# Pre-norm factors applied to the products instead of the operands, post-norm factors made on columns, in a two-layer transformer block kernel

## The chip, the cores and the metric

One core of one Trainium2 chip runs the whole program once. The metric is the device time in microseconds (us). Lower is better. A profiled execution gives the rows quoted here; its span is the time from its first to its last recorded instruction.

## The reference, cut to what matters

The program computes a first block (two layers, 512 tokens, model width 1024) and a second block, of which only its opening, which follows the first, matters here. With `rms_norm(x, g) = x * rsqrt(mean(x*x) + eps) * g` over the 1024 features of a token, the first block is:

```python
for l in range(2):
    g = norm_gains[l]
    if l == 0:
        mix = dilated_mixer(rms_norm(h, g[0]), w_qkv_a[l], w_o_a[l], cos, sin)
    else:
        kvf = rms_norm(h, kv_norm) @ w_kvf          # keys, values, forget gates
        mix = fox_mixer(rms_norm(h, g[0]), w_q_b[0], w_o_b[0], k, v, cumsum(log_sigmoid(f + b_f)))
    h = h + rms_norm(mix, g[1])
    f = conv_ffn(rms_norm(h, g[2]), w_up[l], conv_w[l], conv_b[l], w_down[l])
    h = h + rms_norm(f, g[3])
```

So there are norms ahead of a projection (pre-norms) and norms of a mixer's or a feed-forward's output (post-norms). `conv_ffn` projects to 5632 channels, applies a causal convolution of width 3 along tokens, then gelu(gate) times value, and projects back.

## The kernel before, in words

**Layout.** The residual `h` and every operand of a projection lie feature-major: eight tiles k = 0..7 of 128 features by 512 tokens. A product of fp32 numbers is made of three fp32r matmuls (`hi_lo_product`): operand and weight are each split into a rounded part (hi) and a rest (lo), and hi*hi, hi*lo and lo*hi are summed in PSUM. A matmul of 128x128 weights with 512 columns is the unit of TensorE's work; one output chunk of a projection from 1024 features takes 24 of them.

**Weights.** SyncE loads units of 128x1024 weights into a ring of four; GpSimd (`split_units`, L476 to L484) splits each unit into hi (L482) and lo (L484), in three slots. It may refill a slot once the last product that reads it is done (`product_done`). TensorE takes each unit with a wait on `part_ready`.

**Products.** `fm_linear` gives feature-major chunks in banks f % 4. Where its operand is still being made, it takes the first three chunks together, k by k, as their operand tiles become ready (the lead), and so holds all three weight slots to the lead's end. `tm_linear` gives token-major blocks (values of the attention), unit by unit, two k to a unit, four token blocks in banks 0 to 3.

**Norms.** In a pre-norm ScalarE squares each `h[k]` (`squares`, L580), TensorE sums them over the features with a matmul by ones into bank 7 (`sum_squares`, L610), ScalarE takes the square root (L614), VectorE the reciprocal on 128x512 (L619). Then `norm_dve` makes h * g * rstd (L626), ScalarE rounds it to hi (`split_act`, L499) and VectorE subtracts to lo (`split_dve`, L504). Products start after that. In a post-norm (`out_dve`, `out_act`, `out_pe`) the squares of the mixer's output `mix` are added on VectorE (L598), summed by one matmul (L603), then root and reciprocal as above, and VectorE updates h tile by tile (L674, L678). The matmuls by ones, and the small ones of one column (L1204), are plain fp32.

**Stages.** Attention a (start: `mixa_*`): rotated queries and keys (twelve chunks, each with a rotation matmul L945 of the copy `nb[0:2]` in bank 4 or 5), values, attention, output projection; feed-forward 0; attention b (`mixb_*`): values in two halves b_v0 and b_v1, forget gates b_f, then keys and queries b_kq pair by pair, which also fill gaps of the attention; output projection; feed-forward 1; second block. Each feed-forward has two halves: 22 chunks up (ScalarE tap L719, VectorE taps L740 and L743, gelu, product L749, splits) and eight chunks down over eleven k (`down`, 33 matmuls each), beside which VectorE works at the second block's modulation vectors (L1196, summed by L1204).

**Order.** Every engine's order is written out by hand in these functions; an engine works in that order, and waits on semaphores stand ahead of single instructions. Nothing is scheduled by a planner.

## Time and profile before

| | us |
|---|---|
| median of 3 runs | 2685.9 |
| lowest, highest | 2664.63, 2690.1 |
| time of the profiled execution | 2680.04 |
| its span | 2678.3 |
| TensorE busy in the span | 2370.1 |
| VectorE, ScalarE, GpSimd busy | 1396.6, 591.2, 1105.2 |

The busy times say how full an engine is, not which wait ends last. That is read stage by stage, from the chain of waits and from the order of instructions in time. Granted clock is given as a share of 2.4 GHz. Where a line number is named without more, it is that of the kernel before.

### The profile page before, as it was taken

What the parts mean: (1) busy time and instruction counts of PE and PEld (TensorE: products, weight loads), DVE (VectorE), ACT (ScalarE), POOL (GpSimd) and SP (SyncE); (2) the same over time, 40 slices, a digit from 0 to 9 for tenths busy, and PEclk for the clock granted to TensorE, in tenths of its full rate; (3) what the DMA queues carried; (4) which work ended last, traced back from release to release, by engine and by line L of the source; (5) the groups of instructions that cost most, each with busy time, mean ns of one, the idle gap of its engine ahead of it and who ended that gap; (6) DMA issues with size and microseconds to landing.
All of it is one profiled execution on the core that took longest, in us unless ns stands there. A gap on an engine that the chain in (4) does not pass through costs nothing.

```text
span 2678.3 us, 34115 instructions
## 1 busy us (share of the span) xinstructions
PE 2370.1 (88%) x14068; PEld 1899.8 (71%) x14068; DVE 1396.6 (52%) x2005; ACT 591.2 (22%) x1159; POOL 1105.2 (41%) x632
## 2 busy tenths in 40 slices
PE   7998799999699996999996989658688796899998
PEld 5866588887477774888883567547488785688886
DVE  5455557446733346465566531677945464550431
ACT  2052220121232322210211300302533321210110
POOL 4613367666342222667662103503210024456663
PEclk9999899999799998999997999868888877999999
DMA  4201134335121111334345001102110001222321
GB/s 154 95 24 48 45 97 173 103 110 184 49 71 40 46 34 39 104 133 149 95 163 203 24 16 49 63 1 77 34 49 3 2 1 55 65 93 95 105 93 63
DMA packets 54058, 204.12 MB, mean 76 GB/s; under 512 B 6000, under 2 KB 6128, under 8 KB 52880
## 3 DMA queue, kind: packets, MB, share of 16 engines
q1 hardware_dynamic: 52560, 188.34, 21.5%
q0 software_dynamic: 1344, 13.60, 1.3%
q8 instruction: 112, 1.84, 0.3%
q14 instruction: 42, 0.34, 0.0%
HBM read 197.72 MB, written 4.19 MB: 75 GB/s over the span
## 4 chain that ended last, share of the span: by engine, by line
PE 81%; DVE 14%; ACT 3%; issue 1%; POOL 1%; DMA 0%; DVEq 0%; SPq 0%; POOLq 0%; ACTq 0%
PE bank L493 59%; PE bank L781 3%; PE bank L809 2%; PE bank L610 1%; DVE nb L619 1%; PE bank L1339 1%; PE bank L1359 1%; PE bank L796 1%; PE bank L2020 1%; PE bank L1367 1%; PE bank L2005 1%; DVE nb L1911 1%; PE bank L2262 1%; PE bank L2016 1%; PE bank L785 1%
## 5 line engine op out<-in xcount | busy, mean ns | idle before, releaser
L493 PE MATMUL bank<-xn_r,parts_r 128*128 128x512 f32 (+1 forms) x3104 | 979.5, 394 | 48.5 <-DVE big_r L504 13.2
L493 PE MATMUL bank<-big_r,parts_r 128*128 128x512 f32 x3112 | 900.5, 393 | 1.0 <-POOL parts_r L484 1.0
L482 POOL TENSOR_SCALAR parts_r<-ring 128x1024 fp32r<-128x1024 f32 x297 | 337.4, 1136 | 1193.8 <-PE bank L493 1169.3
L484 POOL TENSOR_TENSOR parts_r<-ring,parts_r 128x1024 fp32r<-128x1024 f32 x297 | 743.2, 2503 | 24.7
L493 PEld LDWEIGHTS bank<-xn_r,parts_r 128*128 128x128 f32 x3104 | 591.9, 193 | 176.4 <-issue 41.6
L493 PEld LDWEIGHTS bank<-big_r,parts_r 128*128 128x128 f32 x3112 | 584.7, 189 | 123.7 <-DVE big_r L504 2.7
L740 DVE SCALAR_TENSOR_TENSOR big<-bank,small,big 128x511 f32<-128x511 f32 x88 | 65.9, 749 | 277.1 <-ACT big L719 277.1
L719 ACT ACTIVATE big<-bank,small 128x512 f32<-128x512 f32 x88 | 68.3, 781 | 497.1 <-PE bank L493 497.1
L2403 DVE TENSOR_TENSOR big<-big 128x512 f32<-128x512 f32 x32 | 82.3, 2573 | 69.9 <-ACT big_r L2384 69.9
L2357 DVE SCALAR_TENSOR_TENSOR h<-bank,vecs,h 128x512 f32<-128x512 f32 x24 | 17.8, 750 | 193.3 <-PE bank L493 193.3
L493 PE MATMUL bank<-parts_r,xn_r 128*128 128x384 f32 x352 | 95.3, 353 | 15.5 <-DVE big L1902 9.6
L2295 POOL TENSOR_TENSOR big<-big 64x384 f32<-64x384 f32 x12 | 9.9, 822 | 216.9 <-PE bank L2047 164.7
L868 DVE CUSTOM_DVE_ANT_0 big<-bank,cst 128x128 f32<-128x128 f32 (+3 forms) x112 | 54.4, 491 | 85.0 <-PE bank L785 48.8
L610 PE MATMUL bank<-nb,base 128*128 128x512 f32 x112 | 64.9, 728 | 35.5 <-ACT nb L580 35.5
L1196 DVE SCALAR_TENSOR_TENSOR big<-cst,vecs,big 128x1024 f32<-128x1024 f32 x42 | 93.7, 2257 | 2.0 <-DMA cst<-mod_w 1.0
L493 PE MATMUL bank<-mix_r,parts_r 128*128 128x512 f32 x224 | 89.0, 398 | 0.0
L781 PE MATMUL bank<-big 64*128 64x128 f32 (+3 forms) x224 | 81.0, 466 | 0.6 <-issue 0.6
L493 PEld LDWEIGHTS bank<-parts_r,xn_r 128*128 128x128 f32 x352 | 67.8, 201 | 17.8 <-DVE big L1902 10.2
L749 DVE TENSOR_TENSOR big<-big 128x512 f32<-128x512 f32 x44 | 79.5, 1806 | 0.8 <-ACT big L726 0.8
L1902 DVE SCALAR_TENSOR_TENSOR big<-bank,small,big 128x488 f32<-128x488 f32 (+5 forms) x108 | 68.3, 636 | 20.5 <-ACT big L1857 17.3
L610 PEld LDWEIGHTS bank<-nb,base 128*128 128x128 f32 x112 | 22.3, 224 | 78.1 <-issue 38.7
L809 PEld LDWEIGHTS bank<-big 128*128 128x128 f32 x560 | 72.6, 191 | 5.1 <-issue 0.4
(349 smaller groups left out, 2985.4 us busy)
## 6 DMA issues: line engine op xcount, KB each, us to landing
ring<-weights SPq DMA_DIRECT2D x297, 512.0 KB, 3.5
...
```

What stands on the lines that cost most here:

```text
L482: pool.tensor_scalar(rounded(w_hi[:, slot]), w, 1.0, 0.0, ALU.mult, ALU.add).then_inc(sem("hi_ready"), 1)
L484: pool.tensor_tensor(rounded(w_lo[:, slot]), w, value(w_hi[:, slot]), ALU.subtract).then_inc(part_ready, 1)
L493: mm = pe.matmul(ps, rounded(w[a]), rounded(x[b]), start=(start and n == 0), stop=(stop and n == 2))
L610: pe.matmul(bank[7][:, :], ones, sq[:, k % 2], start=(k == 0), stop=(k == KD - 1)).then_inc(summed, 1)
L719: act.activation(cv[:, i % 4], bank[i % 4][:, :], ACT.Identity, bias=gain(f"cb{l}", 2 * KH * s + i), scale=gain(f"cw{l}2", 2 * KH * s + i))\
L740: link(dve, dve.scalar_tensor_tensor(out=c[:, 1:T], in0=ps[:, 0:T - 1], scalar=gain(f"cw{l}1", w), in1=c[:, 1:T], op0=ALU.mult, op1=ALU.add))
L749: dve.tensor_tensor(ff_lo[:, j - 1], ge[:, (j - 1) % 2], cv[:, (2 * j - 1) % 4], ALU.mult)\
L781: mm = pe.matmul(ps[:, 0:w], qT[r:r + HD, hd // 2 % ring, tb * P:(tb + 1) * P], kT[r:r + HD, hd // 2 % ring, 0:w], start=True, stop=(sel i ...
L809: mm = pe.matmul(ps[:, g * HD:(g + 1) * HD], PT[:, t % 2, g, kb * P:(kb + 1) * P], vT[:, kb, hd * HD:(hd + 1) * HD], start=(kb == 0), stop ...
L1196: ins = dve.scalar_tensor_tensor(out=acc, in0=w, scalar=c, in1=acc, op0=ALU.mult, op1=ALU.add)
L1902: ins = dve.scalar_tensor_tensor(out=u[:, :, o0:o1], in0=ps[:, :, o0 + s:o1 + s], scalar=gd_tap(kind, f, j), in1=u[:, :, o0:o1], op0=ALU.m ...
L2403: dve.tensor_tensor(ff2_lo[:, f], ff2_lo[:, f], ff2_lo[:, f], ALU.mult).then_inc(sem("mlp_sq"), 1)
```

## The change

- **Pre-norms of the first block.** The operand of a projection is now h * g, without the factor rstd of each token: ScalarE makes hi from h and the gain (`feed_act`), VectorE makes lo = h * g - hi in one instruction (`feed_dve`), for each tile as soon as it is there. The matmuls that sum squares stand between the products (argument `each`): after the three products of each k of a lead, or after each unit of b_v0. The factor is multiplied in behind the product: into the rotation tables of queries and keys of a, into the copies of the values by ScalarE (`token_rs`, one factor per token, made by four small matmuls and a copy), by an instruction of VectorE in place in PSUM for each of the 88 up chunks (`scale`), and for keys, queries and gates of b by VectorE where ScalarE copied before.
- **Post-norms.** The sums of squares are made on columns: four token blocks of one column each, two small matmuls for each; root and reciprocal work on 128x4; four matmuls of a broadcast column by the identity spread it to 128x512 in bank 5, from where VectorE reads it.
- **Order.** In `out_dve` each h[k] is followed by the lo part of tile k - 1. In the up halves VectorE's taps of a chunk follow the scaling of the next. The gates b_f come ahead of b_v1. b_x's hi and lo follow behind the second reciprocal. The first two copies of keys and queries come behind the cumulated gates.

```diff
     out += ffn(0)
     key_query = np.stack([fm_units(wf[:, :D]), fm_units(i["w_q_b"][0])], axis=1).reshape(-1, P, UNIT)
-    out += [("b_v0", tm_units(wf[:, D:D + 512])), ("b_v1", tm_units(wf[:, D + 512:2 * D])),
-            ("b_f", fm_units(pad_cols(wf[:, 2 * D:], [P], B_HEADS))), ("b_kq", key_query),
+    out += [("b_v0", tm_units(wf[:, D:D + 512])), ("b_f", fm_units(pad_cols(wf[:, 2 * D:], [P], B_HEADS))),
+            ("b_v1", tm_units(wf[:, D + 512:2 * D])), ("b_kq", key_query),
             ("b_o", fm_units(i["w_o_b"][0]))]
     out += ffn(1)
...
+        def token_rstd_pe(pe, norm, n):
+
+            pe.wait_ge(rstd_ready, NORMS.index(norm) + 1)
+            grab(pe, 6, sem("token_rs"), n + 1)
+            for tb in range(TB):
+                mm = pe.matmul(bank[6][:, tb:tb + 1], rstd[:, tb * P:(tb + 1) * P], ident[:, 0:1], start=True, stop=True)
+            mm.then_inc(sem("token_rs_ps"), 1)
+
+        def token_rstd_dve(dve, n):
+            dve.wait_ge(sem("token_rs_ps"), n + 1)
+            dve.tensor_copy(token_rs, bank[6][:, 0:TB]).then_inc(sem("token_rs"), 1)
...
+        def post_rstd_pe(pe, st):
+
+            n = POSTS.index(st)
+            ps = grab(pe, 5, *after(st + "_tmp", KD))
+            pe.wait_ge(post_squared, (n + 1) * KD)
+            for tb in range(TB):
+                pe.matmul(ps[:, tb:tb + 1], sq[:, 1, tb * P:(tb + 1) * P], ones[:, 0:1], start=True, stop=False)
+                if tb == 0:
+                    pe.wait_ge(post_added, ADDS * (n + 1))
+                mm = pe.matmul(ps[:, tb:tb + 1], var[:, tb * P:(tb + 1) * P], ones[:, 0:1], start=False, stop=True)
+            mm.then_inc(sem("post_sum"), 1)
+            pe.wait_ge(sem("post_col_rs"), n + 1)
+            for tb in range(TB):
+                mm = pe.matmul(ps[:, tb * P:(tb + 1) * P], col_rs[:, tb:tb + 1].broadcast_to((P, P)), ident, start=True, stop=True)
+            mm.then_inc(sem("post_rs"), 1)
+
+        def post_rstd_act(act, st):
+            act.wait_ge(sem("post_sum"), POSTS.index(st) + 1)
+            act.activation(col_sd, bank[5][:, 0:TB], ACT.Sqrt, bias=gain("eps"), scale=1.0 / D).then_inc(sem("post_sd"), 1)
+
+        def post_rstd_dve(dve, st):
+            n = POSTS.index(st)
+            dve.wait_ge(sem("post_sd"), n + 1)
+            dve.reciprocal(col_rs, col_sd).then_inc(sem("post_col_rs"), 1)
+            dve.wait_ge(sem("post_rs"), n + 1)
...
+        def feed_act(act, src, g, hi, k, ready, done):
+
+            act.wait_ge(*ready)
+            act.activation(rounded(hi[:, k]), src[:, k], ACT.Copy, scale=gain(g, k)).then_inc(sem(done), 1)
+
+        def feed_dve(dve, src, g, hi, lo, k, ready, done):
+            dve.wait_ge(*ready)
+            dve.scalar_tensor_tensor(out=rounded(lo[:, k]), in0=src[:, k], scalar=gain(g, k), in1=value(hi[:, k]),
+                                     op0=ALU.mult, op1=ALU.subtract).then_inc(sem(done), 1)
...
             if half:
-                sum_added(pe, st)
-                for k in range(KD):
-                    sum_squares(pe, st + "n", k)
-
-        def out_act(act, st, mix0=0):
+                post_rstd_pe(pe, st)
+
+        def out_act(act, st, feed, mix0=0):
             for k in range(KD):
                 squares_added(act, st, st + "_mix", k, mix0)
-            rstd_sqrt(act, st)
+            post_rstd_act(act, st)
             for k in range(KD):
+                if feed:
+                    g, (hi, lo), name = feed
+                    feed_act(act, h, g, hi, k, after(st + "_h", k + 1), name + "h")
                 squares(act, st + "n", h, st + "_h", k)
             rstd_sqrt(act, st + "n")
...
-            rstd_recip(dve, st)
+            post_rstd_dve(dve, st)
...
                 if k < KD:
-                    dve.scalar_tensor_tensor(out=tmp[:, k % 2], in0=mix[:, k], scalar=gain(g, k), in1=rstd,
+                    dve.scalar_tensor_tensor(out=tmp[:, k % 2], in0=mix[:, k], scalar=gain(g, k), in1=bank[5][:, :],
                                              op0=ALU.mult, op1=ALU.mult).then_inc(sem(st + "_tmp"), 1)
-                if k:
-                    dve.wait_ge(*after(st + "_tmp", k))
-                    dve.tensor_tensor(h[:, k - 1], h[:, k - 1], tmp[:, (k - 1) % 2], ALU.add).then_inc(sem(st + "_h"), 1)
-                    dve.wait_ge(*after(st + "_h", k))
+                    dve.wait_ge(*after(st + "_tmp", k + 1))
+                    dve.tensor_tensor(h[:, k], h[:, k], tmp[:, k % 2], ALU.add).then_inc(sem(st + "_h"), 1)
+                if k and feed:
+                    fg, (hi, lo), name = feed
+                    feed_dve(dve, h, fg, hi, lo, k - 1, after(name + "h", k), name + "l")
+            dve.wait_ge(*after(st + "_h", KD))
             rstd_recip(dve, st + "n")
...
-                          ready=None if s else (st + "_xnl", 0))
+                          ready=None if s else (st + "_xnl", 0),
+                          each=None if s else lambda k: sum_squares(pe, "bn" if l else "an", k))
...
-
-        def ffn_act(act, l):
+            if l:
+                for k in range(KD):
+                    sum_squares(pe, "ffn1n", k)
...
+            def scale(s, i):
+                dve.wait_ge(*after(f"{st}_up{s}", i + 1))
+                dve.tensor_tensor(bank[i % 4][:, :], bank[i % 4][:, :], rstd, ALU.mult).then_inc(sem(st + "_sc"), 1)
+
+            def conv(s, i):
+                ps, c, w = bank[i % 4], cv[:, i % 4], 2 * KH * s + i
+                dve.wait_ge(*after(st + "_tap", w + 1))
+                link(dve, dve.scalar_tensor_tensor(
+                    out=c[:, 1:T], in0=ps[:, 0:T - 1], scalar=gain(f"cw{l}1", w), in1=c[:, 1:T],
+                    op0=ALU.mult, op1=ALU.add))
+                dve.scalar_tensor_tensor(
+                    out=c[:, 2:T], in0=ps[:, 0:T - 2], scalar=gain(f"cw{l}0", w), in1=c[:, 2:T],
+                    op0=ALU.mult, op1=ALU.add).then_inc(sem(st + "_conv"), 1)
+
+            def gated(s, j):
+                dve.wait_ge(*after(st + "_gelu", KH * s + j + 1))
+                dve.wait_ge(*after(st + "_conv", 2 * KH * s + 2 * j + 2))
+                dve.tensor_tensor(ff_lo[:, j], ge[:, j % 2], cv[:, (2 * j + 1) % 4], ALU.mult).then_inc(sem(st + "_ff"), 1)
...
             for s in range(2):
...
+                for i in range(2 * KH + 6):
+                    j, odd = divmod(i, 2)
+                    if i < 2 * KH:
+                        scale(s, i)
+                    if 1 <= i <= 2 * KH:
+                        conv(s, i - 1)
+                    if not odd and 2 <= j <= KH + 1:
+                        gated(s, j - 2)
+                    if odd and 3 <= j <= KH + 2:
+                        split_dve(dve, ff_lo, ff_hi, ff_lo, j - 3, after(st + "_ffh", KH * s + j - 2), st + "_ffl")
+                out_dve(dve, st, g, feed, half=s, then=lambda f, s=s: mod_products(dve, l, s, f))
...
-                    if take_in:
-                        take_in(act, t)
...
+                    if take_in:
+                        take_in(dve, t)
...
-            for k in range(KD):
-                sum_squares(pe, "in", k)
+
...
             fm_linear(pe, "a_qk", 2 * KA, KD, a_x, "a_qk", "a_raw", ready=("a_xnl", 0),
-                      then=lambda f: rotate(f - 1) if f else None)
+                      then=lambda f: rotate(f - 1) if f else None, each=lambda k: sum_squares(pe, "in", k))
             rotate(2 * KA - 1)
+            token_rstd_pe(pe, "in", 0)
...
+                feed_act(act, h, "g00", a_x[0], k, (h_in[k], 16), "a_xnh")
...
                 dve.wait_ge(h_in[k], 16)
+                feed_dve(dve, h, "g00", *a_x, k, after("a_xnh", k + 1), "a_xnl")
             rstd_recip(dve, "in")
-            norm_dve(dve, "g00", *a_x, "a_xn")
             dve.wait_ge(cst_in, 16)
+            dve.tensor_tensor(rope_c, rope_c, rstd, ALU.mult)
+            link(dve, dve.tensor_tensor(rope_s, rope_s, rstd, ALU.mult))
...
+            token_rstd_dve(dve, 0)
             a_dve(dve)
             flip_dve(dve, "a", *a_oT, KA)
-            out_dve(dve, "a", "g01")
-            norm_dve(dve, "g02", *ffn_x, "ffn0_xn")
             mod_start_dve(dve)
+            out_dve(dve, "a", "g01", ("g02", ffn_x, "ffn0_xn"))
...
-        def kq_take(act, i):
-            act.wait_ge(*after("b_kq", i + 1))
+        def kq_take(dve, i):
+            dve.wait_ge(*after("b_kq", i + 1))
             dst = (b_q if i % 2 else b_k)[:, i // 2 % 2]
-            act.activation(dst, bank[2 + i % 2][:, :], ACT.Copy).then_inc(sem("b_kqt"), 1)
-
-        def kq_take_in(act, t):
+            dve.tensor_tensor(dst, bank[2 + i % 2][:, :], rstd, ALU.mult).then_inc(sem("b_kqt"), 1)
...
-            for n in range(2):
-                tm_linear(pe, f"b_v{n}", 512, token_blocks(b_xkv), TB, "b_v", "b_vt", full0=n * TB,
-                          ready=None if n else "b_xkvl")
+            tm_linear(pe, "b_v0", 512, token_blocks(b_xkv), TB, "b_va", "b_vt", ready="b_xkvl",
+                      each=lambda k: sum_squares(pe, "ffn0n", k))
...
+            token_rstd_pe(pe, "ffn0n", 1)
+            tm_linear(pe, "b_v1", 512, token_blocks(b_xkv), TB, "b_vb", "b_vt", read0=TB)
...
         def mixb_act(act):
-            norm_act(act, *b_xkv, "b_xkv")
-            norm_act(act, *b_x, "b_xn")
+            for k in range(KD):
+                feed_act(act, h, "g10", b_x[0], k, after("ffn0_h", k + 1), "b_xnh")
             for i in range(2 * TB):
-                act.wait_ge(*after("b_v", i + 1))
-                act.activation(b_v[:, i % TB, (i // TB) * 512:(i // TB + 1) * 512], bank[i % TB][:, :], ACT.Copy)\
-                   .then_inc(sem("b_vt"), 1)
+                act.wait_ge(*after("b_vb" if i >= TB else "b_va", i % TB + 1))
+                if i == 0:
+                    act.wait_ge(sem("token_rs"), 2)
+                act.activation(b_v[:, i % TB, (i // TB) * 512:(i // TB + 1) * 512], bank[i % TB][:, :], ACT.Copy,
+                               scale=token_rs[:, i % TB:i % TB + 1]).then_inc(sem("b_vt"), 1)
...
             flip_act(act, "b", b_oT[0], KD)
-            out_act(act, "b")
-            norm_act(act, *ffn_x, "ffn1_xn")
+            out_act(act, "b", ("g12", ffn_x, "ffn1_xn"))
...
             mod_out(dve, 0)
-            norm_dve(dve, "kvg", *b_xkv, "b_xkv")
-            norm_dve(dve, "g10", *b_x, "b_xn")
-            z, az, one = nb[0:B_HEADS, 2], nb[0:B_HEADS, 3], nb[0:B_HEADS, 4]
+            for k in range(KD):
+                feed_dve(dve, h, "g10", *b_x, k, after("b_xnh", k + 1), "b_xnl")
+            token_rstd_dve(dve, 1)
+            z, az, one = nb[0:B_HEADS, 2], nb[0:B_HEADS, 3], nb[0:B_HEADS, 1]
...
             dve.tensor_tensor(c_rows(32, 32 + B_HEADS), z, value(b_c[0:B_HEADS]), ALU.subtract).then_inc(sem("b_c"), 1)
+            for c in range(2):
+                kq_take(dve, c)
...
-            ffn_act(act, 0)
+            ffn_act(act, 0, ("kvg", b_xkv, "b_xkv"))
```

At the start TensorE's queue had all eight sums of squares (L610) ahead of the first product. Before:

```order
L610 MATMUL bank<-nb,base 128x512 x8
L493 MATMUL bank<-xn_r,parts_r 128x512
L493 MATMUL bank<-mix_r,parts_r 128x512
L493 MATMUL bank<-xn_r,parts_r 128x512 x2
L493 MATMUL bank<-mix_r,parts_r 128x512
```

Now the first nine products, three for each of three chunks, stand ahead of one sum of squares (L596 of the changed kernel), and so on for each k:

```order
L496 MATMUL bank<-xn_r,parts_r 128x512 x2
L496 MATMUL bank<-mix_r,parts_r 128x512
L496 MATMUL bank<-xn_r,parts_r 128x512
L596 MATMUL bank<-nb,base 128x512
L496 MATMUL bank<-xn_r,parts_r 128x512
L496 MATMUL bank<-mix_r,parts_r 128x512
```

What moved: the sums are now inside the lead. The same holds at the start of both feed-forwards.

TensorE's queue from the last matmuls of feed-forward 0 into attention b (in the changed kernel L654 spreads the post-norm's factor, L596 sums squares, L613 is the small matmul for the values' factor; `parts_r,big_r` are values, `big_r,parts_r` are feature-major chunks). Before:

```order
L1204 MATMUL bank<-base,big 128x1 x8
L603 MATMUL bank<-nb,base 128x512
L610 MATMUL bank<-nb,base 128x512 x8
L493 MATMUL bank<-parts_r,big_r 128x512 x192
L493 MATMUL bank<-big_r,parts_r 128x512 x48
L493 MATMUL bank<-xn_r,parts_r 128x512
```

Now:

```order
L654 MATMUL bank<-base,norm_cols 128x128 x4
L496 MATMUL bank<-parts_r,big_r 128x512 x24
L596 MATMUL bank<-nb,base 128x512 x2
L496 MATMUL bank<-parts_r,big_r 128x512 x24
L596 MATMUL bank<-nb,base 128x512 x2
L496 MATMUL bank<-parts_r,big_r 128x512 x24
L596 MATMUL bank<-nb,base 128x512 x2
L496 MATMUL bank<-parts_r,big_r 128x512 x24
L596 MATMUL bank<-nb,base 128x512 x2
L496 MATMUL bank<-big_r,parts_r 128x512 x24
L613 MATMUL bank<-base,nb 128x1 x4
L496 MATMUL bank<-parts_r,big_r 128x512 x96
```

What moved: the sums stand two behind each unit of b_v0; the 24 matmuls of b_f stand ahead of b_v1.

VectorE's queue at the end of an up half, behind its last chunk's arrival (L740, L743 and L792, L795 are the taps, L749 and L802 the product of gelu and value, L504 and L507 the lo parts that the down projection waits for). Before:

```order
L740 SCALAR_TENSOR_TENSOR big<-bank,small,big 128x511
L743 SCALAR_TENSOR_TENSOR big<-bank,small,big 128x510
L749 TENSOR_TENSOR big<-big 128x512
L504 TENSOR_TENSOR big_r<-big,big_r 128x512
L749 TENSOR_TENSOR big<-big 128x512
L504 TENSOR_TENSOR big_r<-big,big_r 128x512 x2
```

Now:

```order
L787 TENSOR_TENSOR bank<-bank,nb 128x512
L792 SCALAR_TENSOR_TENSOR big<-bank,small,big 128x511
L795 SCALAR_TENSOR_TENSOR big<-bank,small,big 128x510
L507 TENSOR_TENSOR big_r<-big,big_r 128x512
L792 SCALAR_TENSOR_TENSOR big<-bank,small,big 128x511
L795 SCALAR_TENSOR_TENSOR big<-bank,small,big 128x510
L802 TENSOR_TENSOR big<-big 128x512
L507 TENSOR_TENSOR big_r<-big,big_r 128x512
L802 TENSOR_TENSOR big<-big 128x512
L507 TENSOR_TENSOR big_r<-big,big_r 128x512 x2
```

What moved: the scaling L787, the taps of the chunk before and one more lo part now stand between the last chunk and the inputs that the down projection waits for.

## Rows read from the trace of the kernel before

**Rows 1.** The page: the chain that ended last, shares by engine.

```profile
PE 81%; DVE 14%; ACT 3%; issue 1%; POOL 1%; DMA 0%; DVEq 0%; SPq 0%; POOLq 0%; ACTq 0%
```

**Rows 2.** Timeline, start: start us, us, engine, line, operation, count, idle before.

```profile
20.73 2.34 POOL L484 TENSOR_TENSOR parts_r<-ring,parts_r 128x1024 fp32r<-128x1024 f32 x1
```

**Rows 3.** Chain in order of time, start and feed-forward 0: start us, us, what.

```profile
25.06 16.68 PE bank L493 x66
...
45.75 5.74 PE bank L493 x24
52.34 5.49 PE bank L493 x24
...
289.12 17.68 PE bank L493 x66
```

**Rows 4.** Timeline, VectorE, post-norm of a and pre-norm of feed-forward 0.

```profile
260.56 2.72 DVE L598 TENSOR_TENSOR nb<-nb 128x512 f32<-128x512 f32 x1 [0.69 <-ACT nb L592]
266.08 3.35 DVE L619 RECIPROCAL nb<-nb 128x512 f32<-128x512 f32 x1 [2.80 <-ACT nb L614]
269.46 1.42 DVE L674 SCALAR_TENSOR_TENSOR nb<-mix,small,nb 128x512 f32<-128x512 f32 x2
...
283.33 3.35 DVE L619 RECIPROCAL nb<-nb 128x512 f32<-128x512 f32 x1 [2.80 <-ACT nb L614]
```

**Rows 5.** Timeline, TensorE, first product behind that lead.

```profile
310.57 0.47 PE L493 MATMUL bank<-xn_r,parts_r 128*128 128x512 f32 x1 [2.43 <-POOL parts_r L484]
```

**Rows 6.** Timeline, small matmuls, a small reciprocal, an addition that reads PSUM.

```profile
640.24 1.84 PE L1204 MATMUL bank<-base,nb 128*128 128x1 f32 x16
...
972.72 1.02 PE L910 MATMUL bank<-base,big 128*128 128x128 f32 x4
...
297.36 0.25 DVE L1176 RECIPROCAL vecs<-vecs 128x16 f32<-128x16 f32 x1
...
640.44 0.69 DVE L665 TENSOR_TENSOR mix<-mix,bank 128x512 f32<-128x512 f32 x1 [3.66 <-PE bank L493]
```

**Rows 7.** Timeline, from feed-forward 0 into attention b.

```profile
676.01 1.42 DVE L674 SCALAR_TENSOR_TENSOR nb<-mix,small,nb 128x512 f32<-128x512 f32 x2
...
697.11 23.61 PE L493 MATMUL bank<-parts_r,big_r 128*128 128x512 f32 x96 [8.05 <-DVE big_r L504]
...
705.74 2.71 POOL L484 TENSOR_TENSOR parts_r<-ring,parts_r 128x1024 fp32r<-128x1024 f32 x1
706.12 2.88 DVE L504 TENSOR_TENSOR mix_r<-mix,xn_r 128x512 fp32r<-128x512 f32 x1
...
725.64 24.61 PE L493 MATMUL bank<-parts_r,big_r 128*128 128x512 f32 x96 [4.91 <-ACT big L1079]
...
757.47 0.63 ACT L1087 ACTIVATE nb<-nb 16x512 f32<-16x512 f32 x1 [3.48 <-DVE nb L1106]
...
761.17 0.60 ACT L1039 ACTIVATE big<-bank 128x512 f32<-128x512 f32 x1 [1.13 <-PE bank L493]
...
766.37 0.68 DVE L1118 TENSOR_TENSOR nb_r<-nb,nb_r 16x512 fp32r<-16x512 f32 x1
```

**Rows 8.** Timeline, end of an up half, feed-forward 0.

```profile
602.46 9.84 PE L493 MATMUL bank<-big_r,parts_r 128*128 128x512 f32 x41
603.47 0.75 DVE L740 SCALAR_TENSOR_TENSOR big<-bank,small,big 128x511 f32<-128x511 f32 x1 [3.91 <-ACT big L719]
603.91 2.41 POOL L484 TENSOR_TENSOR parts_r<-ring,parts_r 128x1024 fp32r<-128x1024 f32 x1
604.92 1.95 DVE L749 TENSOR_TENSOR big<-big 128x512 f32<-128x512 f32 x1
608.00 1.47 DVE L504 TENSOR_TENSOR big_r<-big,big_r 128x512 fp32r<-128x512 f32 x2
```

**Rows 9.** Stretches: us, length, busy by engine, granted clock, DMA share, GB/s.

```profile
308.00:313.00 5.00, 2.57 (x8) 1.95 (x8) 4.01 (x6) 0.95 (x2) 4.84 (x3) 0.84 0.31 93
...
988.00:994.00 6.00, 3.57 (x17) 2.66 (x16) 4.06 (x4) 1.69 (x3) 4.92 (x4) 1.00 0.09 24
```

127 lines of the change are left out of this document (52 added, 75 removed).

## The prediction, on record before the changed kernel ran

> **What bounds the kernel now.** I read the page's chain first: 81% of the path to the end is TensorE [rows 1]. The change takes no product away, so it can gain only where TensorE waits for a norm, and each matmul that it puts between products costs its time. So I went to the timeline at each norm and looked at two things: when the first product starts, and what lets the chunk after the lead start. Behind the post-norm of a, VectorE adds the last square at 260.56, takes a reciprocal of 3.35 us, starts on h at 269.46, takes a second reciprocal at 283.33, and TensorE's first product comes at 289.12 [rows 3, 4]. The 72 products of the lead end about 308.2 (66 in 17.68, six more at 0.229), and chunk 3 starts at 310.57, since GpSimd can refill only then [rows 3, 5]. The reader should see that the lead itself is no wait: an earlier start is worth only what is left when the lead's end, GpSimd's refill and VectorE's way to free the bank have moved too.
>
> **Prices.** A product: 0.229 us (24 in 5.49) [rows 3]. A plain fp32 matmul of 512 columns: chunks behind the lead of a start 6.59 us apart with one rotation between, 24 products take 5.5, which leaves 0.9 to 1.1; I take 0.9 for a sum of squares [rows 3]. A lead that starts after idleness loses 2.6 to the lower clock (66 in 17.68 instead of 15.1). An instruction on 128x512 of VectorE costs 0.69 to 0.75, the one that reads PSUM 0.69 even beside GpSimd [rows 6]. With two SBUF operands it took 2.88 where GpSimd was in its subtraction of 2.71 [rows 7]. By the Trainium skill (SBUF — State Buffer, section "SBUF: two separate sides") the two share a pair of ports by an exclusive lock, so the later one waits out the whole of the other's instruction; with that the worst price would be 2.71 + 0.69 = 3.4 and the sum below at most 2 us higher. The row is nearer, I keep 2.88.
>
> **Post-norm on columns.** Now, from the last square (260.5) to h: 8.9 us. Then: eight small matmuls 1.84 (16 records are eight), root and reciprocal about 0.25 each, four spreads of 128 columns 1.02 [rows 6], hand-overs 0.4: 3.8. Saved 5.1; at the lower clock the twelve matmuls take 2.9 more and 2.2 is saved. TensorE was busy until 1.4 us before, so I take 5.
>
> **The two leads of the feed-forwards.** h starts at 264.5. The first lo part comes after two updates of h and itself, about 4.1: first product 268.6. The lead is 72 x 0.229 + 8 x 0.9 + 2.6 = 26.3, TensorE-bound (3.0 per k against 2.2 on VectorE), and ends at 294.9, not 308.2: the eight sums, which now stand inside, take 7.2 of the 20.5 gained at its start. Chunk 0's slot is free 2.3 before that end (six products and the last sum), the refill takes 3.5: chunk 3 at 296.1, 14.5 earlier. The bank for chunk 4 needs root 0.7, reciprocal 3.35, scaling 0.7, tap 0.8, scaling and taps of VectorE 1.6: 302.3 or so, 0.7 after chunk 3's end. The clock fell to 0.84 behind this gap of 2.43 us and stayed at 1.00 behind another of the same length [rows 9]; the new gap is 1.2, so up to 1.5 is gained again. 14.3 for each of two leads: **-28.6** (11 to 17 each).
>
> **The start.** Here the old sums cost nothing: they ran while weights were awaited. GpSimd has the third slot at 23.07 [rows 2], the first product came at 25.06 [rows 3], so only 2 us can be won, against 7.2 of sums inside. 66 products 15.1, sums 7.2, clock 2.6: lead end 48.0 against 43.1. The first two rotations stand ahead of chunk 3 and their copies now wait on the last sum and root (0.8), two copies (1.3) and two rotations (1.8, partly beside): chunk 3 at 51.4 instead of 45.75. Then reciprocal (to 52.2), two table products at 0.7 to 2.9 while GpSimd refills three slots (55.2), the first tile's three instructions (59), a copy (59.7), and only then the rotation of chunk 2: chunk 4 at 60.6 instead of 52.34 [rows 3]. With 1.0 for the values' factor **+9.5** (5 to 13).
>
> **Scaling of the 88 chunks.** 0.69 each, as the row that adds from PSUM [rows 6]; writing PSUM from VectorE has no row, so 0.69 to 2.9, nearest the first. For two chunks (10.9 us of TensorE) VectorE has four taps, a product of 1.95 and a lo part, 5.7 us [rows 8], with scaling 7.1: hidden. It is not hidden at the end of a half. Before, the last two lo parts were done at 609.4, 7.0 after the down projection's start at 602.46, just as its k = 9 and 10 want them (6.2 and 6.9) [rows 8]. Now 0.7 + 1.5 + 0.7 stand ahead (the last order excerpt), the lo part held by GpSimd's subtraction until 606.3; but the product that took 1.95 comes after it and takes 0.7. k = 8 is ready at 609.7, wanted at 607.9; the rest 0.5 more. **+9.2** for four halves (2.3 each; 0 to 4).
>
> **Into attention b.** h starts at 671.0 instead of 676.01 [rows 7]. b_v0's first unit wants two tiles: 677.0, 20 us before now. Unit 0 with clock and two sums ends at 686.9. ScalarE can round tile 2u + 3 only after squaring 2u + 2, which waits for sum 2u: square, rounding, lo part come 2.3 behind that sum, and GpSimd, which refills from the unit's last product on, holds the lo part to 3.5: TensorE idles 2.5 three times (1.3 without the hold). 686.9 + 3 x (2.5 + 7.3) = 716.3, and 0 to 8 for the clock behind each gap, of which I take 4: 720.3, where b_v0 ends now (720.7). b_f follows (5.5). Reciprocal to 724.5, eight lo parts of b_x with one hold (6.5), factor and four copies (2.3): b_v1 at 733.5, not 725.64 [rows 7]; less 5.5 for b_f, +2.4. Behind b_v1 the first copies of keys now stand behind the gates' sum, which ended at 767.05, 16.8 after b_v1, 3.5 of it a wait that falls away [rows 7]: 13.3, with a copy 14, where TensorE wants it at 10.9 (it was at 761.17): +2.7. **+5** (-3 to +11). In the attention VectorE gets 14 copies of 0.7, under a task in four: 0 (-2 to +3).
>
> **End of feed-forward 1.** The small matmuls wait for the modulation's until 1.2 after the square, h's updates no longer overlap: **-1.5**.
>
> **Sum:** -28.6 + 9.5 + 9.2 + 5 - 1.5 = -6.4 from the profiled execution's 2680.04: 2673.6. The median shown is 5.9 above that execution; from it, the same sum gives 2679.5. I say **2676**.
>
> **Rivals.** (1) The forecast, the gain of the leads given back at the start, in b and at four down projections: 50%, 2662 to 2688. (2) The clock holds. If the sums keep TensorE at 2.4 GHz over the short gaps and the lo parts miss GpSimd's turns, into b costs -3, the start +6, down +2, the leads -31: 2680 - 27.5 = 2652.5. For it: the gap at 1.00; against: 0.84 behind an equal one [rows 9]. The Trainium skill (TensorE: Matmul & The Clock Gate, "Part 1") says that the engine's default state is throttled and activity releases it, which speaks for this case where sums fill the lead. 25%. (3) Holds and clock at their upper bounds everywhere: start +13, b +11, down +14, leads -24: 2692.5. 15%. (4) Slower, by one mechanism: the scaling that writes PSUM. It decides from 2.6 us each, where VectorE's 5.7 plus two scalings pass 10.9. At 2.9 a pair takes 11.5, 44 pairs +26, and each down projection waits 2.2 more: 2673.6 + 35 = 2709. Against it: the row that reads PSUM is not held. 6%. (5) The earlier feed brings nothing, since some wait keeps the products behind the reciprocal: the order excerpts speak against it; 2673.6 + 28.6 = 2702. 4%.
>
> **Range and chances.** A comparison here tells about 1% (27 us) from no change. 2648 to 2702 leaves out the far end of (2), half of (4) and what I have not seen. Faster by over 1% of the median (below 2659): most of (2) and a little of (1), 0.25. Slower (above 2713): part of (4) and the unseen, 0.08. Within: 0.67.
>
> **What would show it.** First product of feed-forward 0 about 20 us after the last chunk of a, not 30; chunk 3 37 behind that chunk, not 51. Chunk 4 of the start near 60. In b_v0 three gaps of 1 to 3 us put down to lo parts, and one of some 8 ahead of b_v1, put down to ScalarE's copies. A wait near k = 8 in each half's first down chunk. Scaling at 0.7. I am wrong if scaling is above 1.2, if TensorE waits in the up loops, or if the leads take far from 26 us.

## The result: slower, by products that take 2% longer

| | median us | lowest, highest | ratio to before, 95% interval |
|---|---|---|---|
| before, same comparison (4 runs) | 2675.53 | 2664.63, 2690.1 | |
| changed (4 runs) | 2709.95 | 2704.45, 2717.22 | 1.0116 [1.007, 1.0163] |
| changed, run again beside the experiments (5 runs; before: 26 runs, median 2677.7) | 2705.1 | 2696.45, 2708.43 | 1.0086 [1.0058, 1.0115] |

The forecast was 2676, range 2648 to 2702, with 0.08 on slower by over 1%. The profiled execution of the changed kernel has a span of 2702.7 us, 24.4 above the one before.

**The page and the chain, changed kernel.** The chain's shares hardly moved from [rows 1]:

```profile
PE 82%; DVE 12%; ACT 3%; issue 1%; POOL 1%; DMA 0%; SPq 0%; DVEq 0%; POOLq 0%; ACTq 0%
```

Pieces of it in order of time (start us, us, what):

```profile
26.53 3.12 PE bank L496 x9
...
62.18 7.40 PE bank L496 x24
70.44 5.49 PE bank L496 x24
...
310.51 5.80 PE bank L496 x24
316.32 100.51 PE bank L496 x432
...
2342.23 340.74 PE bank L496 x1464
```

Against [rows 3, 5] the reader should see three things. Chunk 4 of the start comes 8.9 us later: its first product is at 61.19, 52.34 before (the long row at 62.18 lies in it). Chunk 3 of feed-forward 0 comes at the same time, 310.51 against 310.57, so the lead has won back what the start lost. And the last row is the surprise. It is the second block's feed-forward, which the change doesn't touch. The kernel before, same view:

```profile
2303.77 17.29 PE bank L493 x66
2324.84 333.72 PE bank L493 x1464
```

7.0 us are lost there on 1464 products. It is not the clock: two stretches of 40 us inside the first up half, engines' busy times, granted clock, DMA share and GB/s, first before:

```profile
360.00:400.00 40.00, 40.00 (x178) 33.12 (x177) 20.34 (x22) 10.10 (x16) 24.47 (x15) 1.00 0.33 101
```

and changed:

```profile
360.00:400.00 40.00, 40.00 (x174) 32.33 (x174) 29.23 (x28) 10.29 (x16) 24.17 (x14) 1.00 0.31 97
```

TensorE is busy throughout in both, at a granted clock of 1.00, but starts 174 matmuls where it started 178. Read product by product, starts lie 226.7 ns apart before, without exception in the long loops. In the changed kernel they lie 224 to 241 ns apart here, in a pattern that repeats after 15 products, 232 on average. All three kinds of product are slowed alike, though in an up half only the one with the operand's lo part reads `big` (`big_r,parts_r` in a row; the other two read `xn`). Where no operand lies in `big`, as in the projections of attention a (64 to 80 us), the average is 228 in both kernels.

### The profile page after: what moved, and what is told of

Same layout as the page of the kernel before. It is cut to its first block, busy times and chain, and to the rows that moved or that the text cites. A ratio compares the mean times of both kernels' runs of the same rounds, so it can differ in the third digit from the quotient of the medians.

```text
span 2702.7 us, 34373 instructions
## 1 busy us (share of the span) xinstructions
PE 2403.5 (89%) x14172; PEld 1917.9 (71%) x14172; DVE 1463.0 (54%) x2070; ACT 580.4 (21%) x1143; POOL 1101.4 (41%) x632
## 4 chain that ended last, share of the span: by engine, by line
PE 82%; DVE 12%; ACT 3%; issue 1%; POOL 1%; DMA 0%; SPq 0%; DVEq 0%; POOLq 0%; ACTq 0%
PE bank L496 60%; PE bank L843 3%; PE bank L871 2%; PE bank L596 2%; PE bank L1405 1%; PE bank L1425 1%; PE bank L858 1%; PE bank L2086 1%; PE bank L1433 1%; PE bank L2071 1%; DVE nb L1977 1%; PE bank L2328 1%; POOL parts_r L487 1%; PE bank L2082 1%; PE bank L847 1%
## 5 line engine op out<-in xcount | busy, mean ns | idle before, releaser
L496 PE MATMUL bank<-xn_r,parts_r 128*128 128x512 f32 (+1 forms) x3104 | 1003.6, 400 | 51.4 <-POOL parts_r L487 30.2
L496 PE MATMUL bank<-big_r,parts_r 128*128 128x512 f32 x3112 | 915.2, 398 | 12.6 <-DVE big L795 8.9
L787 DVE TENSOR_TENSOR bank<-bank,nb 128x512 f32<-128x512 f32 x88 | 61.3, 699 | 155.9 <-PE bank L496 155.8
L2469 DVE TENSOR_TENSOR big<-big 128x512 f32<-128x512 f32 x32 | 86.7, 2713 | 74.1 <-ACT big_r L2450 74.1
L507 DVE TENSOR_TENSOR big_r<-big,big_r 128x512 fp32r<-128x512 f32 x76 | 105.7, 1393 | 0.4
L802 DVE TENSOR_TENSOR big<-big 128x512 f32<-128x512 f32 x44 | 83.5, 1898 | 0.0
L589 ACT ACTIVATE nb<-h 128x512 f32<-128x512 f32 x56 | 35.1, 627 | 221.6 <-PE bank L596 179.2
L1968 DVE SCALAR_TENSOR_TENSOR big<-bank,small,big 128x488 f32<-128x488 f32 (+5 forms) x108 | 68.3, 636 | 20.4 <-ACT big L1923 17.2
L915 ACT ACTIVATE big<-big,stat 128x128 f32<-128x128 f32 (+3 forms) x112 | 62.0, 555 | 74.6 <-DVE stat L937 74.6
```

Of the source, the lines that this page charges most:

```text
L496: mm = pe.matmul(ps, rounded(w[a]), rounded(x[b]), start=(start and n == 0), stop=(stop and n == 2))
L507: dve.tensor_tensor(rounded(lo[:, k]), x[:, k], value(hi[:, k]), ALU.subtract).then_inc(sem(done), 1)
L787: dve.tensor_tensor(bank[i % 4][:, :], bank[i % 4][:, :], rstd, ALU.mult).then_inc(sem(st + "_sc"), 1)
L802: dve.tensor_tensor(ff_lo[:, j], ge[:, j % 2], cv[:, (2 * j + 1) % 4], ALU.mult).then_inc(sem(st + "_ff"), 1)
L915: act.activation(sbt, sbt, ACT.Exp, bias=nm(t + 1), scale=HD ** -0.5, accum_out=ls(t + 1)[:, g:g + 1]).then_inc(s("probs"), 1)
L1968: ins = dve.scalar_tensor_tensor(out=u[:, :, o0:o1], in0=ps[:, :, o0 + s:o1 + s], scalar=gd_tap(kind, f, j), in1=u[:, :, o0:o1], op0=ALU.m ...
```

## Where the stages stand

The whole time of this program moves by up to 28 us from run to run: 2664.71 to 2692.44 in 26 runs of the kernel before. The traces say where. From the reciprocal behind feed-forward 1 to the next norm's, code that no kernel here changes, the time was between 842.4 and 865.4 us, with TensorE's granted clock at 0.81 to 0.84. The long feed-forward stretch behind it falls in groups, 369.0 to 369.6, 376.4 to 376.8, and one kernel each at 377.4 and 379.1. So I compare stages. "First block" is the start of the reciprocal behind feed-forward 1, "last stretch" the time between the starts of the last two reciprocals on 128x512, all from the profiled execution. Each ratio is to runs of the kernel before taken together with that kernel, with medians of 2675.5 (changed), 2677.7 (before_again to conv_first), 2686.8 (the next three and best1, on another chip) and 2680.3 (before_pad32, weights_off64, post_wide, best2), so medians of different groups can't be compared:

| kernel | median us | ratio, 95% interval | first block | last stretch |
|---|---|---|---|---|
| before | 2675.5 | | 1447.8 | 369.0 |
| before_again | 2686.4 | 0.9996 [0.9966, 1.0027] | 1449.4 | 369.0 |
| changed | 2710.0 | 1.0116 [1.007, 1.0163] | 1458.4 | 376.8 |
| after_again | 2705.1 | 1.0086 [1.0058, 1.0115] | 1459.3 | 376.8 |
| start_old | 2687.4 | 1.0045 [1.002, 1.007] | 1442.3 | 376.4 |
| conv_first | 2693.0 | 1.0054 [1.0025, 1.0083] | 1449.9 | 376.5 |
| after_behind | 2684.2 | 0.9987 [0.9959, 1.0015] | 1437.9 | 369.1 |
| after_cols64 | 2676.1 | 0.9984 [0.9954, 1.0013] | 1437.4 | 369.5 |
| before_pad16 | 2704.6 | 1.0086 [1.0054, 1.0118] | 1454.7 | 376.8 |
| before_pad32 | 2712.0 | 1.0125 [1.0071, 1.0179] | 1458.2 | 377.4 |
| weights_off64 | 2715.0 | 1.0145 [1.0098, 1.0193] | 1464.8 | 379.1 |
| post_wide | 2681.4 | 1.003 [0.9999, 1.006] | 1451.6 | 369.3 |
| best1 | 2661.2 | 0.9927 [0.9899, 0.9955] | 1428.9 | 369.6 |
| best2 | 2647.2 | 0.9891 [0.9838, 0.9944] | 1411.3 | 369.0 |

## Experiments

**before_again**, no edit.

> The kernel before, unchanged. In the first pair of profiles a product of 512 columns started every 0.2267 us in the kernel before and about every 0.231 in the changed one, in the unchanged second block too. Theory A: that spacing belongs to the single execution or the chip, not to the kernel: here the spacing may be either, and runs of this kernel spread over some 25 us. Theory B: it belongs to the program: 0.2267 here again, and all runs of this kernel within 10 us.

**after_again**, no edit.

> The changed kernel, unchanged. Theory A: ratio to before 0.995 to 1.005, and its profile can show 0.2267 between products. Theory B: ratio 1.010 to 1.018 and 0.230 to 0.233 between products again, second block included. Both: chunk 3 of the start at 51, chunk 4 at 61, first down chunks of both feed-forwards 2.2 us late behind the taps of up chunk 20.

Measured: the kernel before spread over 29 us (2665.08 to 2694.23), but its products lay 0.2267 apart in this trace too, and the last stretch took 369.0. The changed kernel had averages of 0.230 to 0.232 and 376.8 again; its ratio of 1.0086 lies between the ranges that I had given for the two theories. So the spread is as theory A has it, and the spacing is as theory B has it: it belongs to the program.

**start_old**: sums ahead of the first product, the old operand, tables and copies unscaled.

```diff
+            for k in range(KD):
+                sum_squares(pe, "in", k)
...
-                      then=lambda f: rotate(f - 1) if f else None, each=lambda k: sum_squares(pe, "in", k))
+                      then=lambda f: rotate(f - 1) if f else None)
...
```

> The changed kernel with the start alone as before (sums of squares ahead of the first product, operand h*g*rstd, unscaled tables and copies of the values). Both theories: attention a starts 12.8 us earlier than in the changed kernel, nothing else moves: 12 to 13 us below it. If the start's cost is partly made good later, less than 9.

Measured: attention a's first row maximum (VectorE's first maximum over scores, the start of the attention) 140.7 against 152.4 and 151.7 (11.3 before their mean), the first block 16.6 shorter than their mean, the ratio 1.0045 against 1.0086. More than the start was won. The other 5 lie behind it, where the instructions of the two kernels are the same: 3.1 of it in feed-forward 0, where start_old has one low stretch of the clock (granted clock 0.50 for 3.4 us at 469.9) and the changed kernel two (6.8 at 482.6, 3.4 at 612.4). The start's own cost varies with the clock too: the six traces with the new form have that row maximum at 148.8 to 152.4, those with the old form (the weights' offset left aside) at 139.6 to 140.8.

**conv_first**: the taps of up chunk 20 ahead of the scaling of chunk 21.

```diff
+                    if i == 2 * KH - 1:
+                        conv(s, i - 1)
                     if i < 2 * KH:
                         scale(s, i)
-                    if 1 <= i <= 2 * KH:
+                    if 1 <= i <= 2 * KH and i != 2 * KH - 1:
```

> The changed kernel with one edit: at the end of each up half the taps of chunk 20 stand ahead of the scaling of chunk 21. My theory: the down projection's first product waits for bank 0, which those taps read; the four gaps of 2.2 us go, and with them the low clock behind three of them (1.7 each): 9 to 14 us below the changed kernel. Rival, the prediction's place: the wait comes from the lo parts at k = 8 to 10, then a wait of 2 us appears there instead and the time falls by under 3 us.

The place in the changed kernel, timeline, end of the first up half (start us, us, engine, line, tiles, count, idle before):

```profile
416.86 0.70 DVE L787 TENSOR_TENSOR bank<-bank,nb 128x512 f32<-128x512 f32 x1 [1.36 <-PE bank L496]
417.46 0.74 DVE L792 SCALAR_TENSOR_TENSOR big<-bank,small,big 128x511 f32<-128x511 f32 x1
...
418.24 0.75 DVE L795 SCALAR_TENSOR_TENSOR big<-bank,small,big 128x510 f32<-128x510 f32 x1
...
419.04 1.19 PE L496 MATMUL bank<-big_r,parts_r 128*128 128x512 f32 x4 [2.23 <-DVE big L795]
```

The scaling L787 is chunk 21's, the two taps are chunk 20's, and the first product of the down projection starts as they end: it wants bank 0, which they read. With the edit, which best1 has as well, TensorE in best1, same view:

```profile
403.09 6.61 PE L496 MATMUL bank<-big_r,parts_r 128*128 128x512 f32 x27 [1.30 <-DVE big L795]
...
409.95 1.28 PE L496 MATMUL bank<-big_r,parts_r 128*128 128x512 f32 x4 [0.24 <-DVE big_r L507]
```

The gap fell from 2.23 to 1.30, not to nothing: the taps now wait for ScalarE's tap, which VectorE's product of 2.16 us had held up. Part of what was won there went at k = 8 to 10, where products stand up to 0.64 us apart for want of lo parts. From chunk 3's tap to the last down addition best1 takes 349.6 and 349.5 us, after_behind 349.6 and 349.6: in this pair, both with `big` in its old place, the edit is worth nothing. In their first halves best1's first down chunk comes 1.5 us earlier, but the low clock behind it is longer (6.8 us at 466.3 against 3.4 at 478.6) and takes 1.6 back. conv_first's first block is 9.0 us shorter than the mean of the changed kernel's two traces: 2.3 ahead of attention a, which the edit can't reach, 1.9 in feed-forward 0 and 5.0 in feed-forward 1. There both traces of the changed kernel have three low stretches of 3.4 us and conv_first has none. Whether the shorter gaps kept the clock up or chance did isn't shown: the two pairs disagree, and the ratios (1.0054 and 1.0086) have intervals that overlap. The place that I had named was right, the rival's was next in line, and the 9 to 14 us that I expected are not shown.

**after_behind**, the one that decides. The change holds a line that its shortened diff doesn't show: it allocates a small tile ahead of `big`. The edit puts it behind:

```diff
-        norm_cols = sb("norm_cols", 16)
-        col_sd, col_rs, token_rs = (norm_cols[:, 4 * n:4 * n + 4] for n in range(3))
         BIG = 20992
         big = two_views("big", BIG)
+        norm_cols = sb("norm_cols", 16)
+        col_sd, col_rs, token_rs = (norm_cols[:, 4 * n:4 * n + 4] for n in range(3))
```

> The changed kernel with one edit: its new 16-column tile norm_cols (64 bytes a partition) is allocated behind the tile big, not ahead of it, so that big begins at byte 126976 of a partition (a multiple of 2048) as in the kernel before, not at 127040. Theory C: products slow down by 2% because their moving operands in big begin off a boundary: 0.2267 us between products again everywhere, 20 to 28 us below the changed kernel, ratio to before 0.996 to 1.001. Rival: the spacing comes from something else in the program (the instructions on PSUM, the longer programs): 0.230 to 0.233 again and no gain.

**before_pad16**: `unused = sb("unused", 16)` behind `stat` in the kernel before.

> The kernel before with an unused tile of 16 columns allocated ahead of big, and no other edit. Theory C: 0.230 to 0.233 between products behind the lead of attention a, ratio 1.007 to 1.012. Rival (the spacing belongs to the change's instructions): 0.2267 and ratio 1.000 within 0.3%.

The chain's piece of the last stretch, after_behind:

```profile
2307.61 333.71 PE bank L496 x1464
```

and before_pad16:

```profile
2340.50 340.74 PE bank L494 x1464
```

The expected pair of opposites: the changed kernel without the offset has the old 333.7, the old kernel with it has the changed kernel's 340.74, and the ratios cross over too, 0.9987 and 1.0086. Both ran on the same other chip; post_wide, with `norm_cols` behind `big` on the first one, has the old spacing and 369.3 as well, so it isn't the chip. By the ratio sixteen unused columns cost as much as after_again measured for the whole change, 23 us. The stages place 13 to 15 of them (5.3 to 6.9 in the first block, 7.8 in the last stretch); the stretch between these varies by 23 us from run to run. In the stretch of 40 us that held 174 matmuls, after_behind has the old number:

```profile
360.00:400.00 40.00, 40.00 (x178) 33.13 (x177) 29.92 (x29) 8.58 (x13) 24.29 (x15) 1.00 0.30 96
```

VectorE is busy for 29.92 of 40 us there, 20.34 before: the scaling isn't what slows the products.

**after_cols64**: `sb("norm_cols", 64)`.

> The changed kernel with norm_cols of 64 columns, so that big begins at byte 127232, a multiple of 256 and not of 512. Theory C with a boundary of 256 bytes or less: as after_behind, 0.2267. With a larger boundary: 0.230 to 0.233 and the changed kernel's time.

**before_pad32**: `sb("unused", 32)`.

> The kernel before with an unused tile of 32 columns ahead of big, which then begins at a multiple of 128 bytes, not of 256. If a boundary of 128 bytes is enough: 0.2267 us between products, ratio 1.000. If it takes 256: 0.228 to 0.233 and a ratio of 1.003 to 1.010.

**weights_off64**, in the kernel before:

```diff
+        unused_a = sb("unused_a", 16)
         parts_all = two_views("parts", 2 * PARTS * UNIT)
+        unused_b = sb("unused_b", 48)
```

> The kernel before with 16 unused columns ahead of the split weights and 48 behind them: the stationary operands begin 64 bytes off a boundary of 256, the moving operands (xn, mix, big) do not. If only the moving operand's place matters: 0.2267 us between products, ratio 1.000. If the stationary one matters too: 0.230 or more from the first product on.

At a multiple of 256 bytes (after_cols64) the spacing was 226.7 ns again. At 128 (before_pad32) it was slow too, in patterns that change from stretch to stretch: 227 to 235, 231 on average, from 361 to 400 us, and 230 to 236, 233 on average, from 1100 to 1180. Its ratio of 1.0125 is above the range that I had given. The last stretch:

```profile
2346.60 341.28 PE bank L494 x1464
```

With the weights 64 bytes off it was 233.3 ns from the first product on, in the projections of attention a too, whose moving operands `xn` and `mix` never moved:

```profile
2349.80 343.38 PE bank L495 x1464
```

So the place of either operand counts, and 256 bytes were enough here. Whether two misplaced operands add up was not tried, and why the place counts was not found.

**best1**: start_old, conv_first and after_behind together.

> The changed kernel with three edits: the start as before, the taps of up chunk 20 ahead of the scaling of chunk 21, norm_cols behind big. If the gains add: 12.8 + 12 + 24 below the changed kernel, ratio to before 0.989 to 0.993. If theory C is wrong: 25 below the changed kernel, ratio 0.998 to 1.002.

Measured 0.9927, first block 1428.9, 9.0 below after_behind. All of it is the start: attention a's first row maximum is at 140.4 against 149.5, and the feed-forwards give nothing, as told above. So the ratio lies in the range given for gains that add, but the stages show no gain of the second edit.

**post_wide**, after_behind with the post-norm's factor on 128x512 again:

```diff
-            for tb in range(TB):
-                pe.matmul(ps[:, tb:tb + 1], sq[:, 1, tb * P:(tb + 1) * P], ones[:, 0:1], start=True, stop=False)
...
+            pe.matmul(ps[:, :], ones, sq[:, 1], start=True, stop=False)
+            pe.wait_ge(post_added, ADDS * (n + 1))
+            pe.matmul(ps[:, :], ones, var, start=False, stop=True).then_inc(sem("post_sum"), 1)
...
-            dve.reciprocal(col_rs, col_sd).then_inc(sem("post_col_rs"), 1)
+            dve.reciprocal(rstd, var).then_inc(sem("post_col_rs"), 1)
```

> The kernel after_behind (the changed kernel with norm_cols behind big) with the post-norms' factor made on 128x512 again: two matmuls by ones, root, reciprocal, no columns. By the prediction's term the columns are worth 5 us a post-norm, less where TensorE is at its lower clock: 16 to 20 us above after_behind. Rival: the columns' small matmuls and hand-overs eat the gain, under 8 us above.

The post-norm of a, timeline, after_behind:

```profile
268.33 0.68 DVE L711 COPY mix<-bank 128x512 f32<-128x512 f32 x1
...
269.82 0.35 PE L647 MATMUL bank<-base,nb 128*128 128x1 f32 x2 [1.56 <-ACT nb L632]
...
273.20 0.18 DVE L664 RECIPROCAL norm_cols<-norm_cols 128x4 f32<-128x4 f32 x1 [4.19 <-ACT norm_cols L659]
273.43 2.08 PE L654 MATMUL bank<-base,norm_cols 128*128 128x128 f32 x8 [0.56 <-DVE norm_cols L664]
275.55 0.75 DVE L718 SCALAR_TENSOR_TENSOR nb<-mix,small,bank 128x512 f32<-128x512 f32 x1 [2.17 <-PE bank L654]
```

and post_wide:

```profile
271.80 0.68 DVE L704 COPY mix<-bank 128x512 f32<-128x512 f32 x1
...
273.28 1.10 PE L646 MATMUL bank<-nb,base 128*128 128x512 f32 x2 [1.57 <-ACT nb L632]
274.22 1.02 PE L648 MATMUL bank<-nb,base 128*128 128x512 f32 x2
...
276.00 3.35 DVE L657 RECIPROCAL nb<-nb 128x512 f32<-128x512 f32 x1 [3.52 <-ACT nb L652]
279.38 0.75 DVE L711 SCALAR_TENSOR_TENSOR nb<-mix,small,nb 128x512 f32<-128x512 f32 x1
```

From the last copy to h it is 7.22 us with columns and 7.58 without. But the two don't run at one clock: in after_behind the granted clock is 0.50 from 270.4 to 284.0, so most of the small matmuls and all spreads run at the lower level (3 us for eight, 2.1 for the spreads), while in post_wide it is 1.00 until 277.3, past both matmuls. after_again has the clock at 1.00 until 278.7, and there the same instructions take 5.18 us:

```profile
273.48 0.69 DVE L711 COPY mix<-bank 128x512 f32<-128x512 f32 x1
...
277.46 1.16 PE L654 MATMUL bank<-base,norm_cols 128*128 128x128 f32 x8 [0.57 <-DVE norm_cols L664]
278.66 0.75 DVE L718 SCALAR_TENSOR_TENSOR nb<-mix,small,bank 128x512 f32<-128x512 f32 x1 [1.25 <-PE bank L654]
```

So columns are worth 2.4 us a post-norm where the clock holds and 0.3 to 0.7 where it falls 2 us behind the copy; post_wide has 7.6 at all four. From the last chunk to the next stage's first product, or at the end of feed-forward 1 to the pre-norm's reciprocal, post_wide takes 0.4, 1.5, 0.7 and 2.5 us more than after_behind at the four post-norms, 5.0 together. Its first block is 13.7 longer. 2.6 of the rest stand ahead of the first post-norm, so no edit made them, and 4.0 in attention b, where post_wide has two low stretches of the clock (6.8 us at 980.4, 3.4 at 1004.3) and after_behind none. I call the columns' worth 5 us in all, not 16 to 20.

**best2**: best1 with three edits of order.

```diff
-            for k in range(KD):
-                if feed:
+            for k in range(-2, KD):
+                if feed and k + 2 < KD:
                     g, (hi, lo), name = feed
-                    feed_act(act, h, g, hi, k, after(st + "_h", k + 1), name + "h")
-                squares(act, st + "n", h, st + "_h", k)
+                    feed_act(act, h, g, hi, k + 2, after(st + "_h", k + 3), name + "h")
+                if k >= 0:
+                    squares(act, st + "n", h, st + "_h", k)
...
+            token_rstd_dve(dve, 0)
             for k in range(KD):
                 feed_dve(dve, h, "g10", *b_x, k, after("b_xnh", k + 1), "b_xnl")
-            token_rstd_dve(dve, 0)
...
+            kq_take(dve, 0)
             dve.wait_ge(*after("b_ln", 1))
...
-            for c in range(2):
-                kq_take(dve, c)
+            kq_take(dve, 1)
```

> The kernel best1 with three edits of order ahead of attention b: ScalarE rounds h two tiles ahead of its squares; VectorE copies the values' factor ahead of b_x's eight lo parts; the first copy of keys stands ahead of the gates' sum. If b_v0's three gaps of 2.6 us come from lo parts held behind the squares' waits, the gap of 9.3 ahead of b_v1 from the copies' factor behind b_x, and the 2.8 from the key copies: attention b starts 15 to 19 us earlier than in best1 (counted from the last chunk of feed-forward 0), ratio to before 0.984 to 0.990. Rival: the weights' split or the clock then sets b_v0, and under 8 us is won.

TensorE in b_v0 and ahead of b_v1, timeline, the changed kernel:

```profile
688.02 7.12 PE L496 MATMUL bank<-parts_r,big_r 128*128 128x512 f32 x24 [6.13 <-DVE big_r L675]
...
699.48 5.84 PE L496 MATMUL bank<-parts_r,big_r 128*128 128x512 f32 x24 [2.62 <-DVE big_r L675]
...
709.65 5.84 PE L496 MATMUL bank<-parts_r,big_r 128*128 128x512 f32 x24 [2.62 <-DVE big_r L675]
...
719.82 5.84 PE L496 MATMUL bank<-parts_r,big_r 128*128 128x512 f32 x24 [2.62 <-DVE big_r L675]
...
742.97 25.32 PE L496 MATMUL bank<-parts_r,big_r 128*128 128x512 f32 x96 [9.30 <-ACT big L1147]
...
782.00 5.99 PE L496 MATMUL bank<-big_r,parts_r 128*128 128x512 f32 x18 [2.74 <-DVE big L1104]
```

and best2:

```profile
665.12 7.37 PE L496 MATMUL bank<-parts_r,big_r 128*128 128x512 f32 x24 [5.75 <-DVE big_r L675]
...
673.65 6.05 PE L496 MATMUL bank<-parts_r,big_r 128*128 128x512 f32 x24
...
705.14 23.63 PE L496 MATMUL bank<-parts_r,big_r 128*128 128x512 f32 x96 [3.04 <-ACT big L1152]
```

The three gaps of 2.6 are gone, 9.3 became 3.0, and the 2.7 at the keys is gone too. From the last addition of feed-forward 0 to attention b's first row maximum it is 91.9 us, 110.6 in best1: 18.7 won, at the upper end of what was expected. best2 at 0.9891 beats both kernels; by the ratio that is 29 us below the kernel before. The three edits were not tried one by one.

## Why the prediction was wrong, step by step

The step that failed stands in the prices: "A product: 0.229 us", taken from the old trace for every product of the new kernel, with the first paragraph's sentence that the change "can gain only where TensorE waits for a norm". I read the change as a list of instructions and never asked where its new tile lies. `big` moved by 64 bytes, and the products of every stage that reads an operand from it came further apart, in stages that the change doesn't touch as well: 232.0 ns instead of 226.7 in the up halves, where one product in three reads `big`, and 229.2 instead of 226.8 in a down projection, where all do. On the last stretch's 1464 products that is 2.1%. None of the five cases had it.

How the loss divides: between the tap of chunk 3 and the last down addition the offset alone makes a feed-forward 4.4 us longer (352.0 in before_pad16, 347.6 before), and the last stretch 7.8. In the changed kernel the same feed-forward stage is 7.6 longer than in after_behind, more than the offset alone. Over the first block the changed kernel and after_again stand 20.4 to 21.9 above after_behind and after_cols64, with the last stretch 28 to 29, against a miss of 29 to 34 from the forecast. before_pad16 stands 5.3 to 6.9 above the kernel before over the first block. The two differ by the clock as well as by the products, as the windows of the first 1400 us show, before_pad16:

```profile
0.00:1400.00 1400.00, 1304.34 (x5825) 0.97 0.28 92
```

before:

```profile
0.00:1400.00 1400.00, 1303.38 (x5854) 0.96 0.28 93
```

(columns: TensorE's busy time, granted clock, DMA share, GB/s): the padded kernel happened to have more of the full clock. Why a stretch falls low in one run and not in the next was not found.

With the offset taken out, the sum can be judged. after_behind and after_cols64 against before and before_again, in us:

| stage | forecast | measured |
|---|---|---|
| start, to attention a | +9.5 | +9.0 |
| attention a and its output | 0 | -0.4 |
| lead of feed-forward 0, to chunk 3's tap | -14.3 | -12.2 |
| rest of feed-forward 0 | +4.6 | +2.0 |
| into attention b | +5 | +5.6 |
| attention b and its output | 0 | -2.7 |
| lead of feed-forward 1 | -14.3 | -11.9 |
| rest of feed-forward 1 | +4.6 | +2.0 |
| end of feed-forward 1 | -1.5 | -2.3 |
| sum | -6.4 | -10.9 |

By the whole time the two kernels without the offset stand at 0.9987 and 0.9984, 3.5 to 4.3 us below the kernel before, and both intervals (0.28% to either side of one, 0.30% of the other) hold 1. So the forecast of a small gain is borne out by the stages and not by the whole time, which is too uncertain for it.

- **Start.** Chunk 3 began at 50.85 in the changed kernel (forecast 51.4) and chunk 4 at 61.2 (60.6). The wait before the rotation was 3.3 us, and the granted clock was 0.53 from 59 to 66, for which I had no term. Of the six traces with this start the four with such a low stretch have the first row maximum at 149.7 to 152.4, the two without at 148.8 and 149.5: it cost up to 3 us.
- **Post-norm.** The size depends on the clock. From the last copy to h it was 10.27 us before, and I had 5.3 at 264.5. Where the clock held through it (after_again above) it was 5.18, as forecast; where it fell two microseconds behind the copy, as in both attentions' post-norms of after_behind, 7.22 and 6.92, so 3.1 saved, nearer the 2.2 that I had worked out for the lower clock and set aside than the 5 that I took. Against post_wide's 7.6, 2.7 of what was won come from the last square, which is no longer added on VectorE (2.72, [rows 4]), and 0.4 to 2.4 from the columns. I had booked all of it to the columns.
- **Leads.** In the kernels without the offset the first product came 10.7 to 11.1 us behind the last copy, 29.7 to 30.3 before: 19 of the forecast 20.5. The lead with its sums takes 25.9 to 26.3, 19.0 to 19.4 before, 6.8 longer (forecast 7.2). The gap ahead of chunk 3 fell from 2.43 to 1.54, forecast 1.2, and the low clock behind it [rows 9] went, worth 1.6 on the up half (97.9 to 96.4). It counts in the table's next stage; with it a lead gave 13.5 to 13.8 against 14.3.
- **Scaling.** 0.70 each, hidden in the loops. The minimum, median and maximum in ns, changed kernel, the scaling's line:

```profile
L787 DVE TENSOR_TENSOR bank<-bank,nb x88: 689/700/700, 313.2 to 1371.4; 128x512 f32<-128x512 f32 x88
```

- **Down starts.** Size near, place wrong. From chunk 21's tap to the first down chunk it took 2.8 us longer where a low clock followed the gap and 1.35 where none did (forecast 2.3). I had the wait at k = 8 behind lo parts; it stood at the first product behind the taps of chunk 20, and at k = 8 only once these had gone ahead (conv_first). I had counted what stands ahead of the lo parts and not what stands ahead of the bank.
- **Attention b.** Gaps of 2.62, 2.62, 2.62 (forecast 2.5), 9.3 ahead of b_v1 ("some 8"), 2.74 at the keys (2.7): this step was right in place and size. The lo parts in these gaps took 1.96 beside GpSimd's subtraction. In best1 one began at 677.17, GpSimd's ran from 676.23 for 2.35. By the Trainium skill (SBUF — State Buffer, section "SBUF: two separate sides") the later one waits for the whole of the other's instruction, which gives an estimate of 1.41 + 0.69 = 2.1; the trace agrees within 0.15. My 2.88 for any start was too much.
- **Rivals.** Rival 4's end on the slower side was right, and its mechanism, a slow scaling, wrong. Rivals 2 and 3 were about the clock; without the offset the sum by stages (2680.0 - 10.9 = 2669.1) lies between the forecast's 2673.6 and rival 2's 2652.5.

On where operands start, the Trainium skill (SBUF — State Buffer, section "Operand start alignment") says that an operand must start at a multiple of its element size, and adds: "This is about legality, not speed". All offsets here are legal, multiples of 64 bytes with elements of 4; what they cost in speed is what these runs measure.
